# Filter generation in a diffusion-trunk kernel: the middle sample's spreading matmuls replaced by one spread per group, and absolute values of sample tiles added on GpSimd

## The chip, the cores and the metric

The kernel runs on one core of a Trainium2 chip. Five engines work side by side and meet through semaphores: TensorE (PE in the trace) multiplies matrices, VectorE (DVE), ScalarE (ACT) and GpSimd (POOL) work on tiles of 128 partitions, and SyncE (SP) issues the transfers between memory and the core. The metric is the device time of one execution in microseconds (us), the median of several runs.

## The reference, cut to what matters

The whole trunk is one layer for two request groups (a prompt of 256 rows, a sample of 1024): modulation, a projection, neighbourhood attention beside a long convolution, an output projection, and a routed mixture of experts. Only the first part of the kernel is touched: it makes the spectra of the convolution's filters, for both lengths and both orders.

```python
def implicit_filter_fft(length, w1, b1, w2, b2, w3, freq):
    ...
    hid = jnp.sin(fr * (z @ w1 + b1))
    hid = jnp.sin(fr * (hid @ w2 + b2))
    filt = (hid @ w3).reshape(length, 2, HYENA_ORDER, D_HYENA)
    filt = filt * window[:, None, None, :]
    fwd, bwd = filt[:, 0], filt[:, 1]
    two_sided = jnp.concatenate([fwd, zeros, bwd[1:][::-1]], axis=0)
    two_sided = two_sided / jnp.sum(jnp.abs(two_sided), axis=0, keepdims=True)
    return jnp.fft.rfft(two_sided, axis=0)
```

The spectrum also takes up the convolution's skip term (`hyena_bias`), since adding `u * bias` after the convolution is adding the bias to each cosine coefficient.

## The kernel before

The kernel is a row of phases with a barrier between them: filters, projection, attention, convolution (`hyena`), mixing and routing, experts. The filters phase fills the span's first 324 us and the projection starts after its barrier; nothing of the projection runs before that.

Inside `filters` each engine has a fixed program, written out by hand, and runs it in order. Its pieces:

- **Units** 0 to 9 are tiles of filter samples: for order 0 unit 0 is the prompt (t = -1) and 1 to 4 the sample (t = 0 to 3); for order 1 they are 5 and 6 to 9. For a unit, PE makes four 128x512 results (`gen`), DVE multiplies them by the window tile (`windowed`, into `AB`; with three small operations more where t is 0 or -1), POOL adds and subtracts `AB` into the operand tile `opnd` (three operations, `s_pool`), DVE adds one more (`odd_sine`), ACT takes two absolute values (`absolute`, into `MA` and `MB`), and DVE takes the larger of them (`larger`, into `MA`). `MA` and `MB` are one buffer each.
- **Sums.** For each unit PE multiplies `MA` by a matrix of ones and accumulates in `pn` (`sums`, two matmuls). `close` adds the middle sample's share. DVE takes the reciprocal of `pn` (`inverse`, into `rn`). There are four groups: order 0 prompt (0), order 0 sample (1), order 1 prompt (2), order 1 sample (3). ACT may overwrite `MA` only when PE has summed it.
- **Spectra.** Group g has jobs j: 5 for a prompt, 17 for the sample; below, spectrum 1/6 is job 6 of group 1. PE multiplies the basis table by `opnd` (one matmul for a prompt, four for a sample) into `pk`, which has two buffers. For jobs whose coefficients see the middle sample (3 of 5, 9 of 17) PE adds two matmuls of one row each, a rounded part `mid_h` and a rest `mid_l` times the signs `sgn`. DVE (`spectrum_out`) scales `pk` by `rn`, for cosines adds the skip term in a second operation, and writes `spec`, also of two buffers, which SP stores; DVE waits for the store before the last. PE waits for DVE's job before the last.
- **Ada.** Between these, 24 steps of the modulation: SP loads 1 MB, PE multiplies, DVE copies out. PE's step waits for DVE's last one.

On PE the order is gen 2, sums 1, ada, spectra 0/0 to 0/4, gen 3, sums 2, ada, gen 4, sums 3, ada, sums 4, close 1, then spectra 1/0 to 1/16 with gen 5 to 9 after jobs 0, 3, 6, 9, 12 (`GEN_AT`), sums 5 to 9 after jobs 2, 5, 8, 11, 14 (`SUM_AT`) and close 2 and 3 after jobs 2 and 14; then groups 2 and 3. SP loads a window tile only in its turn between the stores (`win_load`), behind an ada load and a table load.

## Time and profile before

| | us |
|---|---|
| median of three runs | 3416.4 |
| lowest and highest | 3412.28, 3417.86 |
| profiled execution, device time | 3407.46 |
| its span in the trace | 3405.7 |

The profile shows one execution; its device time is 1.8 us above its span and 8.9 us under the median. Over the whole span PE is busy 94%, DVE 65%, ACT 49% and GpSimd 11%. The trace gives each instruction's start and duration from the span's start. An idle time in brackets names what ended it. The granted clock is TensorE's, as a share of 2.4 GHz: 1.00 is 2.4 GHz, 0.50 is 1.2 GHz. A float32 matmul is two records in the trace, one of the rounded type is one.

### The profile page before, as it was taken

Reading aid. Unit: us, or ns where it says so; the run is one execution under the profiler, and the core shown is the slowest. Engines: PE = TensorE matmul, PEld = TensorE weight load, DVE = VectorE, ACT = ScalarE, POOL = GpSimd, SP = SyncE. Lnnn points to the kernel's source line nnn. Section 1 sums busy time; section 2 is a strip of 40 time slices with the busy share of each in tenths; the row PEclk is TensorE's granted clock in tenths of the full one; section 3 lists DMA queues with packets and bytes.
Section 4 is the critical chain, followed back from the end, with each engine's and each line's share of the span. In section 5 each row is a group of like instructions: output and inputs, shape, how many; then the busy total and the mean of one; then the engine's idle time right before and its main releaser. Section 6 shows DMA issues by size and latency. Waiting matters only on the chain.

```text
span 3405.7 us, 54105 instructions
## 1 busy us (share of the span) xinstructions
PE 3194.1 (94%) x22270; PEld 2430.2 (71%) x22270; DVE 2196.7 (65%) x2820; ACT 1655.7 (49%) x2154; POOL 373.3 (11%) x316
## 2 busy tenths in 40 slices
PE   4898999979899894999999999999999999999996
PEld 2443788878778773777777777777777777777774
DVE  6643333167666547777777777777777777777775
ACT  1102322156412333666666666666666666666663
POOL 1210100011244131000000000000000000000010
PEclk8999999989999896999999999999999999999998
DMA  3465342254676434788778778777777777777785
GB/s 138 182 221 195 99 128 94 72 146 126 223 245 218 150 101 165 278 299 293 273 289 298 274 285 295 275 288 289 278 289 281 281 291 280 285 283 289 277 325 200
DMA packets 226034, 791.14 MB, mean 232 GB/s; under 512 B 28525, under 2 KB 35321, under 8 KB 221564
## 3 DMA queue, kind: packets, MB, share of 16 engines
q1 hardware_dynamic: 206028, 722.02, 57.3%
q0 software_dynamic: 19760, 65.65, 6.7%
q8 instruction: 177, 2.90, 0.3%
q14 instruction: 69, 0.57, 0.0%
HBM read 730.31 MB, written 57.26 MB: 231 GB/s over the span
## 4 chain that ended last, share of the span: by engine, by line
PE 58%; DMA 1%; DVE 1%; ACT 0%; issue 0%; POOL 0%; SPq 0%; ACTq 0%; POOLq 0%; DVEq 0%
PE exp_bank L2779 15%; PE exp_bank L2781 14%; PE exp_bank L2780 14%; PE exp_bank L2789 14%; PE exp_bank L2761 1%; DMA out_y<-exp_xb 1%; PE exp_bank L2763 1%; DMA exp_xb<-residual 0%; PE exp_bank L2747 0%; DVE g_pick L2342 0%; DVE g_pick L2341 0%; DVE g_pick L2344 0%; DVE exp_lo L2475 0%; DMA exp_xq<-hidden_rows,g_rows_q 0%; PE exp_bank L2751 0%
## 5 line engine op out<-in xcount | busy, mean ns | idle before, releaser
L2475 DVE TENSOR_TENSOR exp_lo<-exp_raw,exp_hi 128x1024 fp32r<-128x1024 f32 x1056 | 1277.4, 1223 | 249.4 <-ACT exp_hi L2471 191.0
L2471 ACT ACTIVATE exp_hi<-exp_raw 128x1024 fp32r<-128x1024 f32 x1056 | 1119.2, 1061 | 572.0 <-PE exp_bank L2781 558.4
L2779 PE MATMUL exp_bank<-exp_hi,exp_xt 128*128 128x512 f32 (+1 forms) x1536 | 588.6, 383 | 1.3 <-DVE exp_xt L2628 1.0
L2781 PE MATMUL exp_bank<-exp_hi,exp_xt 128*128 128x512 f32 (+1 forms) x1536 | 571.9, 372 | 0.0
L2780 PE MATMUL exp_bank<-exp_lo,exp_xt 128*128 128x512 f32 (+1 forms) x1536 | 571.4, 372 | 0.0
L2779 PEld LDWEIGHTS exp_bank<-exp_hi,exp_xt 128*128 128x128 f32 x1536 | 289.4, 188 | 86.9 <-issue 39.1
L2781 PEld LDWEIGHTS exp_bank<-exp_hi,exp_xt 128*128 128x128 f32 x1536 | 289.6, 189 | 52.0
L2789 PE MATMUL exp_bank<-exp_raw,exp_xtp 128*32 128x256 f32 (+1 forms) x6144 | 324.1, 363 | 0.0
L2780 PEld LDWEIGHTS exp_bank<-exp_lo,exp_xt 128*128 128x128 f32 x1536 | 290.2, 189 | 45.4
L2779 PE MATMUL exp_bank<-exp_hi,exp_hid 128*128 128x512 f32 x704 | 283.7, 403 | 10.4 <-DVE exp_lo L2475 10.4
L2781 PE MATMUL exp_bank<-exp_hi,exp_hid 128*128 128x512 f32 x704 | 275.8, 392 | 0.0
L2789 PEld LDWEIGHTS exp_bank<-exp_raw,exp_xtp 128*32 128x32 f32 x6144 | 185.2, 110 | 127.0 <-issue 30.9
L2780 PE MATMUL exp_bank<-exp_lo,exp_hid 128*128 128x512 f32 x704 | 275.3, 391 | 0.0
L503 PE MATMUL proj_bank<-proj_hh,proj_hi 128*128 128x512 f32 (+1 forms) x480 | 170.0, 354 | 2.0 <-DVE proj_lo L126 2.0
L504 PE MATMUL proj_bank<-proj_hl,proj_hi 128*128 128x512 f32 (+1 forms) x480 | 170.0, 354 | 0.0
L2779 PEld LDWEIGHTS exp_bank<-exp_hi,exp_hid 128*128 128x128 f32 x704 | 132.6, 188 | 52.3 <-issue 16.3
L505 PE MATMUL proj_bank<-proj_hh,proj_lo 128*128 128x512 f32 (+1 forms) x480 | 169.8, 354 | 0.0
L2789 PE MATMUL exp_bank<-exp_raw,exp_hidp 128*32 128x256 f32 x2816 | 162.3, 381 | 0.0
L2520 POOL TENSOR_TENSOR exp_step<-g_ident 1x1 f32<-1x1 f32 x16 | 4.0, 250 | 1422.3 <-PE exp_bank L2751 1391.1
L2781 PEld LDWEIGHTS exp_bank<-exp_hi,exp_hid 128*128 128x128 f32 x704 | 132.7, 188 | 28.8
L2780 PEld LDWEIGHTS exp_bank<-exp_lo,exp_hid 128*128 128x128 f32 x704 | 132.9, 189 | 25.5
L1167 PE MATMUL filt_pk<-filt_opnd,filt_table 128*128 128x512 f32 x292 | 136.9, 611 | 8.2 <-DVE filt_spec L1379 8.0
(407 smaller groups left out, 4294.0 us busy)
## 6 DMA issues: line engine op xcount, KB each, us to landing
exp_raw<-in_w SPq DMA_DIRECT2D x1056, 512.0 KB
hy_table<-in_basis_s POOLq DMA_DIRECT2D x64, 512.0 KB
carry_tiles<-in_w_ada SPq DMA_DIRECT2D x24, 1024.0 KB, 5.6
proj_raw<-in_w_in SPq DMA_DIRECT2D x24, 512.0 KB
filt_table<-in_kbasis_s SPq DMA_DIRECT2D x18, 512.0 KB, 6.3
spectrum_s<-filt_spec SPq DMA_DIRECT2D x34, 256.0 KB, 2.4
carry_flex<-spectrum_s SPq DMA_DIRECT2D x16, 512.0 KB
features<-proj_xr SPq DMA_DIRECT2D x12, 512.0 KB, 3.0
```

What stands on the lines that cost most here:

```text
L503: pe.matmul(out, whi, hh[:, k, c0:c0 + w], start=(k == 0), stop=False)
L504: pe.matmul(out, whi, hl[:, k, c0:c0 + w], start=False, stop=False)
L505: mm = pe.matmul(out, wlo, hh[:, k, c0:c0 + w], start=False, stop=(k == KT - 1))
L1167: mm = pe.matmul(pk[n % 2][:], table[:, c % NR, ti * 128:(ti + 1) * 128], opnd[:, at, x, :], start=(t == 0), stop=(t == nt - 1 and not rank1))
L2471: act.activation(st.hi[:, n % st.ns, :], raw(n), ACT.Copy).then_inc(st.hi_done, 1)
L2475: dve.tensor_tensor(st.lo[:, n % st.ns, :], raw(n), st.hi[:, n % st.ns, :].bitcast(F32), ALU.subtract).then_inc(st.lo_done, 1)
L2761: pe.transpose(turn_s[:, i * 128:(i + 1) * 128], hd[:, i * 128:(i + 1) * 128], g["ident"][:])
L2763: tr = pe.transpose(turn_p[:, i * 128:(i + 1) * 128], hdp[:, i * 128:(i + 1) * 128], g["ident"][:])
L2779: pe.matmul(out, xh, wh, start=(k == 0), stop=False)
L2780: pe.matmul(out, xh, wl, start=False, stop=False)
L2781: mm = pe.matmul(out, xl, wh, start=False, stop=(k == nk - 1))
L2789: mm = pe.matmul(banks(e * NU + i)[2][q * CAP_P:(q + 1) * CAP_P, 0:w], x[:, k, :], raw(e * NC + c)[:, base + q * w:base + q * w + w], star ...
```

## The change

The middle sample is no longer added by PE in each job. Instead, once, eight float32 matmuls of one row (`middle_rows`) spread it for the four groups into `pk`, ACT copies each result into `spread`, and DVE multiplies it by `rn` and adds the skip term to its cosine half (`fold`, three operations a group). `spectrum_out` then adds the folded tile instead of the skip term; sine jobs that see the middle sample get a second operation that they did not have. For sample units t = 1 to 3 GpSimd adds `MA` to a running total (`totals`), which unit t = 0 starts, and PE sums each group once (sums 0, 4, 5, 9). Sums 4 and close 1 move behind spectrum 1/0.

```diff
+    SUM_AT = {2: 5, 14: 9}
     CLOSE_AT = {2: 2, 14: 3}
...
             def sums(n):
                 gi = group(n)
-                first = n == 0 or group(n - 1) != gi
-                pe.wait_ge(s_MA, n + 1)
-                if first and gi:
+                if UNITS[n][1] < 0:
+                    src = MA
+                    pe.wait_ge(s_MA, n + 1)
+                else:
+                    src = totals[UNITS[n][0]]
+                    pe.wait_ge(s_acc, adds(n))
+                if gi:
                     pe.wait_ge(s_rn, gi)
                 for m in range(2):
-                    mm = pe.matmul(pn[:], g["ones"][:], MA[:, m, :], start=(first and m == 0), stop=False)
+                    mm = pe.matmul(pn[:], g["ones"][:], src[:, m, :], start=(m == 0), stop=False)
                 mm.then_inc(s_sum, 1)
 
             def close(gi):
                 if gi == 0:
                     pe.wait_ge(s_ma, 1)
                 pe.matmul(pn[:], g["ones"][ones_at(gi), :], mid_a[ones_at(gi), :], start=False, stop=True).then_inc(s_n, 1)
+
+            def middle_rows():
+                pe.wait_ge(s_mf, 4)
+                for k in range(8):
+                    gi, x = divmod(k, 2)
+                    if k >= 2:
+                        pe.wait_ge(s_spo, k - 1)
+                    pe.matmul(pk[k % 2][:], sgn[ones_at(gi), :], midf[ones_at(gi), x, :], start=True, stop=True).then_inc(s_sp, 1)
...
-                rank1 = with_middle(q, j)
                 nt = MT if q else 1
                 for t in range(nt):
                     ti, at = ((j % 2) * MT + t, o * PER + 1 + t) if q else (j, o * PER)
                     mm = pe.matmul(pk[n % 2][:], table[:, c % NR, ti * 128:(ti + 1) * 128], opnd[:, at, x, :],
-                                   start=(t == 0), stop=(t == nt - 1 and not rank1))
-                if closes(q, j):
-                    mm.then_inc(s_used, 1)
-                    if not rank1:
-                        return
-                if rank1:
-                    gi, s = 2 * o + q, int(kind == "sin")
-                    pe.matmul(pk[n % 2][:], sgn[ones_at(gi), :], mid_h[ones_at(gi), s, :], start=False, stop=False)
-                    mm = pe.matmul(pk[n % 2][:], sgn[ones_at(gi), :], mid_l[ones_at(gi), s, :], start=False, stop=True)
-                mm.then_inc(s_k, 1)
+                                   start=(t == 0), stop=(t == nt - 1))
+                mm.then_inc(s_used if closes(q, j) else s_k, 1)
...
             gen(2)
-            sums(1)
+            middle_rows()
             ada()
             for j in range(NJ[0]):
                 spectrum(0, 0, j)
             gen(3)
-            sums(2)
             ada()
             gen(4)
-            sums(3)
             ada()
-            sums(4)
-            close(1)
             for j in range(NJ[1]):
                 spectrum(0, 1, j)
+                if j == 0:
+                    sums(4)
+                    close(1)
                 if j in GEN_AT:
                     gen(GEN_AT[j])
...
@@ -1248,8 +1258,11 @@
                 for s, out in enumerate((MA, MB[:])):
                     act.wait_ge(s_AB, 2 * n + s + 1)
                     if n:
-                        act.wait_ge(s_sum, n)
                         act.wait_ge(s_MA, n)
+                        if UNITS[n - 1][1] < 0:
+                            act.wait_ge(s_sum, 1 if n == 1 else 3)
+                        elif added(n - 1):
+                            act.wait_ge(s_acc, adds(n - 1))
...
             absolute(0)
             absolute(1)
-            act.wait_ge(s_mf, 4)
-            act.activation(mid_h[:], midf[:], ACT.Copy).then_inc(s_mh, 1)
+            for k in range(8):
+                act.wait_ge(s_sp, k + 1)
+                act.activation(spread[:, k // 2, k % 2, :], pk[k % 2][:], ACT.Copy).then_inc(s_spo, 1)
             for n in range(2, len(UNITS)):
                 absolute(n)
...
                     if s == 0:
                         ins = pool.tensor_tensor(opnd[:, n, 1, :], AB[:, 0, :], AB[:, 1, :], ALU.subtract)
                     ins.then_inc(s_pool, 1)
+                if added(n):
+                    pool.wait_ge(s_MA, n + 1)
+                    if adds(n) % (MT - 1) != 1:
+                        pool.wait_ge(s_acc, adds(n) - 1)
+                    pool.tensor_tensor(totals[UNITS[n][0]], totals[UNITS[n][0]], MA, ALU.add).then_inc(s_acc, 1)
...
             def larger(n):
                 dve.wait_ge(s_abs, 2 * n + 2)
-                dve.tensor_tensor(MA, MA, MB[:], ALU.max).then_inc(s_MA, 1)
+                first = UNITS[n][1] == 0
+                dve.tensor_tensor(totals[UNITS[n][0]] if first else MA, MA, MB[:], ALU.max).then_inc(s_MA, 1)
 
             def inverse(gi):
                 dve.wait_ge(s_n, gi + 1)
                 if gi == 0:
                     dve.wait_ge(s_mf, 4)
                 dve.reciprocal(rn[:, gi, :], pn[:]).then_inc(s_rn, 1)
+                if gi:
+                    fold(gi)
+
+            def fold(gi):
+                if gi == 0:
+                    dve.wait_ge(s_skip, 32)
+                dve.wait_ge(s_rn, gi + 1)
+                dve.wait_ge(s_spo, 2 * gi + 2)
+                dve.tensor_tensor(spread[:, gi, 0, :], spread[:, gi, 0, :], rn[:, gi, :], ALU.mult).then_inc(s_fold, 1)
+                dve.tensor_tensor(spread[:, gi, 1, :], spread[:, gi, 1, :], rn[:, gi, :], ALU.mult).then_inc(s_fold, 1)
+                dve.wait_ge(s_fold, 3 * gi + 1)
+                dve.tensor_tensor(spread[:, gi, 0, :], spread[:, gi, 0, :], skip[:, gi // 2, :], ALU.add).then_inc(s_fold, 1)
...
+                if kind != "sin" or with_middle(q, j):
+                    if not with_middle(q, j):
+                        term = skip[:, o, :]
+                    else:
+                        dve.wait_ge(s_fold, 3 * (2 * o + q) + 3)
+                        term = spread[:, 2 * o + q, int(kind == "sin"), :]
                     chain(ins)
-                    ins = dve.scalar_tensor_tensor(spec[:, n % 2, :], skip[:, o, :], col, spec[:, n % 2, :], ALU.mult, ALU.add)
+                    ins = dve.scalar_tensor_tensor(spec[:, n % 2, :], term, col, spec[:, n % 2, :], ALU.mult, ALU.add)
                 ins.then_inc(s_ev, 1)
...
-            dve.wait_ge(s_mh, 1)
-            dve.tensor_tensor(mid_l[:], midf[:], mid_h[:].bitcast(F32), ALU.subtract).then_inc(s_ml, 1)
             inverse(0)
             ada()
             unit(2)
             ada()
+            fold(0)
             for j in range(NJ[0]):
                 spectrum_out(0, 0, j)
```

Three places where the order of instructions changes, as they stand on their engines.

ScalarE, between the absolute values of unit 1 and those of unit 2 (`filt_hid` holds `MA`), before:

```order
L1256 ACTIVATE filt_hid<-filt_AB 128x1024 [waits filt_abs_ready,filt_abs_summed,filt_ab_ready]
L1256 ACTIVATE filt_MB<-filt_AB 128x1024 [waits filt_abs_ready,filt_abs_summed,filt_ab_ready]
L1271 ACTIVATE filt_mid_h<-filt_spec 128x1024 [waits filt_mid_ready]
L1256 ACTIVATE filt_hid<-filt_AB 128x1024 [waits filt_abs_ready,filt_abs_summed,filt_ab_ready]
L1256 ACTIVATE filt_MB<-filt_AB 128x1024 [waits filt_abs_ready,filt_abs_summed,filt_ab_ready]
```

and now:

```order
L1269 ACTIVATE filt_hid<-filt_AB 128x1024 [waits filt_abs_summed,filt_abs_ready,filt_ab_ready]
L1269 ACTIVATE filt_MB<-filt_AB 128x1024 [waits filt_abs_summed,filt_abs_ready,filt_ab_ready]
L1285 ACTIVATE filt_spread<-filt_pk 128x512 [waits filt_mid_spread] x8
L1269 ACTIVATE filt_hid<-filt_AB 128x1024 [waits filt_abs_ready,filt_ab_ready]
L1269 ACTIVATE filt_MB<-filt_AB 128x1024 [waits filt_abs_ready,filt_ab_ready]
```

Eight copies from PSUM stand ahead of unit 2's absolute values, where one copy from SBUF stood; the wait for PE's sums is gone there.

GpSimd, from unit 3's third operation on, before:

```order
L1285 TENSOR_TENSOR filt_opnd<-filt_AB 128x512 [waits filt_ab_ready] x2
L1287 TENSOR_TENSOR filt_opnd<-filt_AB 128x512
L1285 TENSOR_TENSOR filt_opnd<-filt_AB 128x512 [waits filt_ab_ready] x2
L1287 TENSOR_TENSOR filt_opnd<-filt_AB 128x512
L1285 TENSOR_TENSOR filt_opnd<-filt_AB 128x512 [waits filt_ab_ready] x2
```

and now (`filt_opnd<-filt_opnd,filt_hid` is the add into the total):

```order
L1299 TENSOR_TENSOR filt_opnd<-filt_AB 128x512 [waits filt_ab_ready]
L1307 TENSOR_TENSOR filt_opnd<-filt_opnd,filt_hid 128x1024 [waits filt_abs_added,filt_abs_ready]
L1299 TENSOR_TENSOR filt_opnd<-filt_AB 128x512 [waits filt_ab_ready]
L1301 TENSOR_TENSOR filt_opnd<-filt_AB 128x512
L1299 TENSOR_TENSOR filt_opnd<-filt_AB 128x512 [waits filt_ab_ready]
```

An add of 128x1024 that waits for DVE's maximum now stands between one unit's operations and the next one's; the same holds for units 2, 4, 7, 8 and 9.

TensorE, at the first sample spectrum (1/0, line 1167 before and 1187 now), before:

```order
L1141 MATMUL filt_pn<-filt_hid,g_ones 128x512 [waits filt_abs_ready]
L1141 MATMUL filt_pn<-filt_hid,g_ones 128x512
L1147 MATMUL filt_pn<-g_pick,g_ones 128x512
L1167 MATMUL filt_pk<-filt_opnd,filt_table 128x512 [waits filt_odd_sine,filt_spec_ready,filt_mixed,filt_table_landed1]
L1167 MATMUL filt_pk<-filt_opnd,filt_table 128x512 x3
L1175 MATMUL filt_pk<-filt_mid_h,filt_sgn 128x512
L1176 MATMUL filt_pk<-filt_mid_l,filt_sgn 128x512
```

and now:

```order
L1187 MATMUL filt_pk<-filt_opnd,filt_table 128x512 [waits filt_odd_sine,filt_spec_ready,filt_mixed,filt_table_landed1]
L1187 MATMUL filt_pk<-filt_opnd,filt_table 128x512 x3
L1154 MATMUL filt_pn<-filt_opnd,g_ones 128x512 [waits filt_rnorm,filt_abs_added]
L1154 MATMUL filt_pn<-filt_opnd,g_ones 128x512
L1160 MATMUL filt_pn<-g_pick,g_ones 128x512
L1128 MATMUL filt_pf<-filt_W,filt_hs 128x512 [waits filt_ab_ready,filt_hid_lo]
```

The sum and the closing matmul of group 1 now follow spectrum 1/0 where they preceded it, and DVE's reciprocal, which ends in `rn` for job 1/0, follows them.

## Rows read from the trace of the kernel before

**Rows 1.** Top line of the page: the profiled span.

```profile
span 3405.7 us, 54105 instructions
```

**Rows 2.** Busy by stretch: length, engines' us, granted clock, DMA.

```profile
122.27:160.38 38.11, 36.30 (x141) 16.91 (x140) 29.37 (x35) 4.01 (x4) 10.57 (x6) 1.00 0.37 131
160.38:232.56 72.18, 69.87 (x259) 31.53 (x255) 38.07 (x60) 6.35 (x6) 15.54 (x9) 1.00 0.60 216
232.56:317.65 85.09, 83.50 (x343) 37.06 (x342) 25.92 (x63) 8.39 (x14) 0.00 (x0) 0.96 0.57 204
```

**Rows 3.** Timeline of PE, 175 to 181: start, duration, line, tiles, idle before.

```profile
175.00 1.88 PE L1141 MATMUL filt_pn<-filt_hid,g_ones 128*128 128x512 f32 x4
176.72 3.60 PE L1167 MATMUL filt_pk<-filt_opnd,filt_table 128*128 128x512 f32 x8
180.25 0.49 PE L1175 MATMUL filt_pk<-filt_mid_h,filt_sgn 1*128 1x512 f32 x1
...
180.89 0.50 PE L1119 MATMUL filt_pf<-filt_W,filt_hs 128*128 128x512 f32 x1
```

**Rows 4.** Groups by line: the middle's spreading matmuls, over the whole run.

```profile
L1175 PE MATMUL filt_pk<-filt_mid_h,filt_sgn 1*128 1x512 f32 x24 | 12.1, 506 | 0.0
```

**Rows 5.** Groups by line, then two timeline rows: nearest prices of added work.

```profile
L1968 POOL TENSOR_TENSOR carry_flex<-carry_flex 128x1024 f32<-128x1024 f32 x10 | 23.8, 2379 | 160.0 <-DVE carry_flex L2098 160.0
L2557 ACT ACTIVATE exp_xt<-exp_bank 128x512 fp32r<-128x512 f32 x32 | 17.2, 585 | 26.4 <-PE exp_bank L2747 26.4
77.23 0.69 DVE L1415 TENSOR_TENSOR g_pick<-filt_spec,g_pick 128x512 f32<-128x512 f32 x1
88.44 1.06 ACT L1256 ACTIVATE filt_hid<-filt_AB 128x1024 f32<-128x1024 f32 x1 [11.61 <-PE filt_pn L1141]
```

**Rows 6.** Timeline of POOL and PE around the last unit before spectrum 1/0.

```profile
113.79 1.28 POOL L1285 TENSOR_TENSOR filt_opnd<-filt_AB 128x512 f32<-128x512 f32 x1 [3.18 <-DVE filt_AB L1340]
...
116.72 2.24 POOL L1285 TENSOR_TENSOR filt_opnd<-filt_AB 128x512 f32<-128x512 f32 x1
117.90 3.39 PE L1141 MATMUL filt_pn<-filt_hid,g_ones 128*128 128x512 f32 x4 [2.49 <-DVE filt_hid L1355]
121.22 1.12 PE L1147 MATMUL filt_pn<-g_pick,g_ones 1*128 1x512 f32 x2
122.27 3.70 PE L1167 MATMUL filt_pk<-filt_opnd,filt_table 128*128 128x512 f32 x8
```

**Rows 7.** Timeline of DVE: first group, first sample spectra, units 5 and 6.

```profile
92.09 0.74 DVE L1376 SCALAR_TENSOR_TENSOR filt_spec<-filt_pk,filt_rowf,filt_rn 128x512 f32<-128x512 f32 x1
...
98.43 0.75 DVE L1376 SCALAR_TENSOR_TENSOR filt_spec<-filt_pk,filt_rowf,filt_rn 128x512 f32<-128x512 f32 x1 [4.16 <-DMA spectrum_p<-filt_spec]
...
110.83 1.23 DVE L1355 TENSOR_TENSOR filt_hid<-filt_hid,filt_MB 128x1024 f32<-128x1024 f32 x1 [1.36 <-ACT filt_MB L1256]
...
122.38 3.36 DVE L1361 RECIPROCAL filt_rn<-filt_pn 128x512 f32<-128x512 f32 x1 [4.07 <-PE filt_pn L1147]
...
128.12 2.47 DVE L1340 TENSOR_TENSOR filt_AB<-filt_pf,filt_win 128x512 f32<-128x512 f32 x4
...
133.83 2.17 DVE L1355 TENSOR_TENSOR filt_hid<-filt_hid,filt_MB 128x1024 f32<-128x1024 f32 x1
...
145.89 2.48 DVE L1340 TENSOR_TENSOR filt_AB<-filt_pf,filt_win 128x512 f32<-128x512 f32 x4 [0.80 <-DMA filt_win<-in_win_s]
```

**Rows 8.** Granted clock in short stretches, and the PE row after the idle.

```profile
101.00:104.00 3.00, 3.00 (x7) 1.36 (x6) 0.91 (x2) 0.00 (x0) 0.00 (x0) 0.50 0.40 152
...
107.00:110.00 3.00, 3.00 (x25) 1.35 (x23) 2.44 (x3) 1.21 (x2) 3.00 (x3) 0.98 0.27 112
...
100.02 1.85 PE L1167 MATMUL filt_pk<-filt_opnd,filt_table 128*128 128x512 f32 x2 [3.71 <-DVE filt_spec L1379]
```

**Rows 9.** Timeline of DVE where a store has to land first.

```profile
229.26 0.75 DVE L1376 SCALAR_TENSOR_TENSOR filt_spec<-filt_pk,filt_rowf,filt_rn 128x512 f32<-128x512 f32 x1 [1.79 <-DMA spectrum_p<-filt_spec]
...
296.25 0.75 DVE L1376 SCALAR_TENSOR_TENSOR filt_spec<-filt_pk,filt_rowf,filt_rn 128x512 f32<-128x512 f32 x1 [6.61 <-DMA spectrum_s<-filt_spec]
```

25 lines of the change are left out of this document (14 added, 11 removed).

## The prediction

> **What bounds the kernel now.** I read the page's top line first: the profiled span is 3405.7 us [rows 1] of a device time of 3407.46. The filters phase ends before the next phase starts, so only this phase can move the time, and what it gains or loses at its end goes straight into the total. Then the table by stretch [rows 2]: from the first sample spectrum (1/0, at 122.27) to 160.38 PE is busy 36.3 of 38.1 us, from there to the end of group 2 69.9 of 72.2, and to the last spectrum 83.5 of 85.1, at a granted clock of 1.00, 1.00 and 0.96. PE bounds these 195 us. But DVE is busy 29.4 us of the first 38.1, so it is the next bound there, and the timeline shows how tight it is: unit 6 on DVE waits for its window tile [rows 7], and a store holds DVE up twice [rows 9]. Ahead of 122.27 PE waits for others: 3.71 us before spectrum 0/4 [rows 8], 2.49 before sums 4 [rows 6].
>
> **What the change takes off PE.** A pair of the middle's matmuls takes 0.64 us of PE (180.25 to 180.89) and a unit's sum 1.72 (175.00 to 176.72) [rows 3]. There are 24 pairs [rows 4], 3 of them in group 0, so 21 after 122.27: 13.4 us. Sums 6, 7 and 8 go too: 5.2. Taken at face value that is 18.6 us of a stretch that PE bounds. What follows walks the new program through, to see how much of it arrives.
>
> **Until spectrum 1/0: +3.3 us.** After gen 2, at 86.3, PE runs eight float32 matmuls of one row. The nearest rows are close's, 1.05 us each (121.22 to 122.27) [rows 6], and a spectrum's, 0.9 (3.60 for four) [rows 3]: 7.2 to 8.4, I take 7.6, till 93.9. The eight ACT copies (0.59 each [rows 5]) follow two buffers behind and hide under them, but the last ends at 94.5, and unit 2's absolute values, which stand behind them on ACT, come then: two of 1.06 [rows 5], the maximum (1.23 [rows 7]), the ada copy (0.5). Now fold 0: three operations of 0.69 [rows 5], which meet GpSimd's add of unit 2 (2.38 alone [rows 5]). Reading both operands from SBUF they wait for it; between none and all of it I take all: 102.2, where job 0/0 began at 92.09 [rows 7]. Part returns: DVE waited 4.16 for the first store then [rows 7], behind loads that are now over, and 2.4 should do. So spectrum 0/4 starts on PE at 107.7 instead of 100.02 [rows 8]; gen 3, without its pair, is 6.5 late. Sums 2 and 3 are gone, and unit 3's maximum ends at 117.7, where it was 112.06 (110.83 plus 1.23) [rows 7]. Here GpSimd gets into the path: its add for unit 3 runs until 120.3, and only then do unit 4's three operations start. They took 5.2 (113.79 to 118.96) [rows 6], so they end at 125.6, and spectrum 1/0 waits for them. Before, it started at 122.27 [rows 6].
>
> **From 1/0 to 1/6: +11.8 to +18.** Sums 4 and close 1 now come after spectrum 1/0: 3.6, 1.8 and 1.05 [rows 3, 6], so DVE's reciprocal starts at 132.1, not at 122.38 [rows 7]. It takes 3.36, fold 1 adds 2.1, job 1/0 1.5, so unit 5 starts at 139.2 where it was 128.12, 11.1 late [rows 7]. DVE needs 7.8 us for it (128.12 to 135.9) [rows 7] and is done at 147.0. PE meanwhile does gen 5, 1/1, ada and 1/2 until 142.9 and must then wait 4.2 us for unit 5's maximum, since sums 5 stands after 1/2. Then sum, close, 1/3: 153.6. Unit 6 needs its window tile, whose load SP issues behind an ada load and a table load; the gap from those to its arrival is the one that ended at 145.89 [rows 7], 8.8 us, and gives 156.8. Unit 6 takes 7.8, reciprocal and fold 5.5, the ada copy 0.5: 170.6. PE's ada step after 1/5 waits for that copy, idle since 164.1, and 1/6 starts at 172.2 with job 1/4 done. Before: 160.38, so +11.8.
>
> The clock can add to it. After PE had idled 3.71 us it stood at 0.50, 1.2 GHz, from 101 to 104 and was back at 0.98 from 107 on [rows 8]: some 7 us of work at half speed. After 2.49 us of idle the two matmuls of sums 4 took 3.3 (117.90 to 121.22) [rows 6] for the usual 1.7. The new program has three gaps, of 5.9 us (119.7 to 125.6), 4.2 and 4 to 6.5. Each should cost what these two did, 1.6 to 3.4. Two of them lie on the chain whole, and of the third 1.4: up to +18, the window's lateness then hidden.
>
> **From 1/6 to the end of group 2: -0.6 to +0.7.** Here 4.5 us of pairs and 3.5 of sums leave PE, out of 72.2 [rows 2]. But units 7 to 9 wait on DVE for window tiles (as at 145.89 [rows 7]) whose loads follow PE's and DVE's steps by the same 7 to 9 us, so DVE comes due 0.7 to 0.9 us after PE twice. Sums 9 waits for GpSimd: unit 9's three operations (5.2 [rows 6]) and then the add of 2.38 [rows 5] end 16.7 us after PE's ada step ahead of 1/12, where the sum stood at 14.6; that is 2.1 lost, not 0.6 gained. Fold 3 (2.1) falls between job 1/15 and job 1/16, and the prompt's jobs 2/0 to 2/4 go at the pace of stores [rows 9]; their four pairs (2.6) bring nothing, and DVE is 0.9 later. Sum: 71.6 for 72.2; with a slow clock at its start an estimated 1.3 more.
>
> **From there to the end: -4.5.** Nine pairs, 5.8 us, and DVE's additions (four operations of 0.75) have room. The stall at 296.25, where the first store behind six loads of 512 KB lands [rows 9], keeps its time and takes 1.3 of it back. The tail is unchanged.
>
> **Sum.** 11.8 - 0.6 - 4.5 = +6.7 at the low end, 18 + 0.7 - 4.5 = +14.2 at the high end. I take +11, nearer the high one, since rows 6 and 8 show the clock down after shorter gaps than the new ones. The profiled execution would go from 3407.5 to 3418.5, the median from 3416.4 to 3427.4.
>
> A rule against the change: the Trainium skill, "GPSIMD Engine Reference", section "4.1 Engine selection", wants two-input elementwise work on VectorE, GpSimd being about half as fast. The trace has 2.38 us for such an operation on GpSimd [rows 5] and 1.23 for the same size on DVE [rows 7]. With the adds on DVE the wait at 120.3 would be about 1.2 us shorter, and the result would be nearer +10.
>
> **The rivals.**
> *PE's relief arrives (faster).* If the waits of DVE, SP and GpSimd that I placed are slack in fact, the stretch after 122.27 shrinks by 18.6, by 1.8 of idle before sums 6, and gives back 1.3 at the loads, while 1/0 starts 3.3 late: -15.8, 3400.6. It decides at unit 5: it holds if the 11.1 us by which DVE is later there are made good before 1/6. For it: PE is 95% to 98% busy after 122.27 [rows 2]. Against: DVE is at 77% in the first stretch, and it gets 4.3 us more of folds just there.
> *The clock stays up (hardly slower).* If no gap lowers it, +6.7: 3423.1. Against it: rows 6 and 8.
> *The two cancel.* If only unit 5's lateness arrives and the loads and adds of 1/6 to 2/4 cost nothing, +6.7 less 5 to 7: about 3416 to 3418.
> *More contention.* If GpSimd's add also stops the second operation of cosine jobs and stretches DVE's folds each time (up to 2.38 for each of six adds), and every gap costs 3.4: +20 to +24, 3438.
> *It doesn't do what it says.* The instruction order shows pairs and sums gone, so none of the chance is here.
>
> **How the numbers follow.** 0.2% of the median is 6.8 us, about what a measurement of this kernel can tell from no change. Chances: forecast 0.50 (+7 to +15), clock stays up 0.12, cancel 0.15, relief arrives 0.14, more contention 0.09. Slower by over 0.2% (above 3423.2): all but a little of the first, all of the last, a little of the second: 0.60. Within it: 0.26. Faster: 0.14. The range leaves out the relief and the far end of the contention: 3408 to 3437. Of it, 3423 to 3431 is the forecast's own.
>
> **What would show it.** In the profile after: spectrum 1/0 on PE at about 125.6 (122.27 before); a wait of PE for DVE's maximum or GpSimd's add at sums 5 and sums 9; PE idle before the ada step ahead of 1/6, which should start at 172 to 178; PEclk under 1.00 between 125 and 185; the last spectrum's end at 324 to 332 instead of 317.65. The forecast is wrong if 1/6 starts before 165, or if PE shows no idle between 1/2 and sums 5; then the relief has arrived.

## The result, and the profile after

The changed kernel takes 3427.5 us (median of 6 runs, 3424.2 to 3434.3) against 3413.3 (6 runs, 3411.5 to 3417.9): a ratio of 1.0042, with a 95% interval of 1.0029 to 1.0055. That is slower by 14 us. The prediction started from a median of 3416.4 (3 runs); with six runs it is 3413.3. The profiled execution took 3430.9 us with a span of 3429.1. I profiled each kernel a second time later: before took 3416.1 there and the changed one 3426.9.

How far can one trace be trusted? In both traces of before the last spectrum ends at 317.7, though the executions differ by 8.6 us. That difference arose behind this phase, where no version changes anything: from the end of the last spectrum to the end of the execution before took 3089.8 and 3098.4 us, the changed kernel 3091.5 and 3090.8. What sets this scatter stays open. The end of the last spectrum on PE is therefore the sharper measure of what the phase costs, and the table goes by it. The columns between are the starts of DVE's three big reciprocals, one behind each of close 1, 2 and 3; they divide the phase in four.

| kernel | 1/0 on PE | recip 1 | recip 2 | recip 3 | last spectrum ends |
|---|---|---|---|---|---|
| before, two traces | 122.3 / 119.5 | 122.4 / 119.6 | 153.7 / 151.0 | 217.8 / 215.1 | 317.7 / 317.7 |
| after, two traces | 127.3 / 127.5 | 136.8 / 136.3 | 171.4 / 170.6 | 242.1 / 243.7 | 339.4 / 336.1 |

By the means of two, the change is 15.6 us late at recip 1, 18.6 at recip 2, 26.4 at recip 3, and 20.0 at the end: the last stretch is the only one that gains. The phase thus loses 20 us where the medians lose 14.

The windows that answer to [rows 2] (columns as there: length; PE, weight loads, DVE, ACT, POOL busy; granted clock, DMA share, GB/s) run from the old start of 1/0 to the new, to 1/6, to the end of group 2, to the last spectrum:

```profile
122.27:127.28 5.01, 0.00 (x0) 0.03 (x1) 2.65 (x5) 1.91 (x2) 5.01 (x4) 0.50 0.83 314
127.28:179.51 52.23, 43.67 (x137) 18.95 (x137) 33.03 (x41) 4.01 (x4) 12.75 (x7) 0.83 0.26 91
179.51:257.40 77.89, 67.20 (x244) 30.92 (x244) 47.73 (x68) 6.35 (x6) 22.91 (x12) 0.90 0.56 202
257.40:339.35 81.95, 77.41 (x320) 35.13 (x308) 28.49 (x67) 8.38 (x14) 0.00 (x0) 0.94 0.60 212
```

PE was busy 36.3 of 38.1 us between 1/0 and 1/6 at a clock of 1.00. Now it is busy 43.7 of 52.2, at 0.83: there is less work in the stretch, and it has both more idle time and longer matmuls. DVE's busy time from 1/6 to the end of group 2 rose from 38.1 to 47.7, with eight instructions more: fold 3's three (2.1 us) and five second operations of sine jobs at 0.75. That is 5.8 of the 9.7; the rest is waiting inside instructions, of which the next rows show cases.

The timeline of PE at its gaps (start, duration, line, tiles, idle before and what ended it):

```profile
86.23 10.17 PE L1168 MATMUL filt_pk<-filt_spec,filt_sgn 1*128 1x512 f32 x16
...
127.28 6.70 PE L1187 MATMUL filt_pk<-filt_opnd,filt_table 128*128 128x512 f32 x8 [5.71 <-POOL filt_opnd L1299]
...
151.43 3.78 PE L1154 MATMUL filt_pn<-filt_hid,g_ones 128*128 128x512 f32 x4 [4.01 <-DVE filt_hid L1375]
...
177.16 0.61 PE L1105 MATMUL filt_pa<-filt_sel,g_pick 128*128 128x2 f32 x4 [4.34 <-DVE g_pick L1324]
```

These are the three gaps the prediction named: ahead of 1/0, ahead of sums 5, and ahead of the ada step before 1/6. Spectrum 1/0 took 6.70 us where it took 3.70 before [rows 6]. The first row is the eight spreading matmuls, at 10.17 us instead of the 7.6 I had put down.

The timelines of GpSimd and of DVE at the first add, and DVE at two later ones:

```profile
100.26 2.34 POOL L1307 TENSOR_TENSOR filt_opnd<-filt_opnd,filt_hid 128x1024 f32<-128x1024 f32 x1 [9.56 <-DVE filt_hid L1375]
100.56 2.59 DVE L1390 TENSOR_TENSOR filt_spread<-filt_spread,filt_rn 128x512 f32<-128x512 f32 x1
140.18 0.69 DVE L1390 TENSOR_TENSOR filt_spread<-filt_spread,filt_rn 128x512 f32<-128x512 f32 x1
...
195.08 2.17 DVE L1415 SCALAR_TENSOR_TENSOR filt_spec<-filt_kz,filt_rowf,filt_spec 128x512 f32<-128x512 f32 x1
198.58 0.75 DVE L1415 SCALAR_TENSOR_TENSOR filt_spec<-filt_spread,filt_rowf,filt_spec 128x512 f32<-128x512 f32 x1
```

The fold's multiplication takes 0.69 alone and 2.59 while the add runs: it ends at 103.15, half a microsecond behind the add's end at 102.60. The second operation of a cosine job, 0.75 alone, takes 2.17 in the same way, and 2.83 at 209.97. Both read two operands from SBUF. (The Trainium skill, "SBUF — State Buffer", section "Who interferes with whom", says that a DVE instruction with two SBUF inputs contends with a GpSimd instruction that reads SBUF, and that the port pair they share is an exclusive lock; these rows agree.)

A stopped operation also holds up transfers, since SP issues its work in order. The timelines of SP and POOL, then of PE at sums 9:

```profile
197.27 0.33 SPq L1028 DMA_DIRECT2D spectrum_s<-filt_spec  x1
197.65 0.43 SPq L1014 DMA_DIRECT2D filt_win<-in_win_s  x1
...
229.33 2.79 POOL L1307 TENSOR_TENSOR filt_opnd<-filt_opnd,filt_hid 128x1024 f32<-128x1024 f32 x1
...
232.17 3.62 PE L1154 MATMUL filt_pn<-filt_opnd,g_ones 128*128 128x512 f32 x4 [2.45 <-POOL filt_opnd L1307]
```

The operation that started at 195.08 ends at 197.25; only then can its store go, and the window load of unit 8 is issued behind that store. The load of unit 9 follows, at 215.69, the store of the one stopped at 209.97. Unit 9's maximum ends at 228.24; its add, which stands behind three other operations on GpSimd, ends 3.9 us later, and sums 9 wait for it.

### The profile page after: what moved, and what is told of

Same layout as the page of the kernel before. It is cut to its first block, busy times and chain, and to the rows that moved or that the text cites. A ratio compares the mean times of both kernels' runs of the same rounds, so it can differ in the third digit from the quotient of the medians.

```text
span 3429.1 us, 54057 instructions
## 1 busy us (share of the span) xinstructions
PE 3199.8 (93%) x22214; PEld 2434.6 (71%) x22214; DVE 2215.9 (65%) x2841; ACT 1658.4 (48%) x2159; POOL 388.3 (11%) x322
## 4 chain that ended last, share of the span: by engine, by line
PE 59%; DVE 1%; DMA 1%; ACT 0%; POOL 0%; issue 0%; SPq 0%; ACTq 0%; POOLq 0%; DVEq 0%
PE exp_bank L2814 15%; PE exp_bank L2816 14%; PE exp_bank L2815 14%; PE exp_bank L2824 14%; PE exp_bank L2796 1%; DMA out_y<-exp_xb 1%; PE exp_bank L2798 1%; PE exp_bank L2782 0%; DVE g_pick L2377 0%; DVE g_pick L2376 0%; DVE g_pick L2379 0%; DMA exp_xq<-hidden_rows,g_rows_q 0%; DMA exp_xb<-residual 0%; PE exp_bank L2786 0%; POOL exp_xg L2556 0%
## 5 line engine op out<-in xcount | busy, mean ns | idle before, releaser
L2816 PEld LDWEIGHTS exp_bank<-exp_hi,exp_xt 128*128 128x128 f32 x1536 | 289.9, 189 | 52.2
L504 PE MATMUL proj_bank<-proj_hl,proj_hi 128*128 128x512 f32 (+1 forms) x480 | 170.6, 355 | 0.0
L1187 PE MATMUL filt_pk<-filt_opnd,filt_table 128*128 128x512 f32 x292 | 150.0, 665 | 18.7 <-DVE filt_spec L1415 13.0
```

The costliest lines, as they stand in the source:

```text
L504: pe.matmul(out, whi, hl[:, k, c0:c0 + w], start=False, stop=False)
L1187: mm = pe.matmul(pk[n % 2][:], table[:, c % NR, ti * 128:(ti + 1) * 128], opnd[:, at, x, :], start=(t == 0), stop=(t == nt - 1))
L2816: mm = pe.matmul(out, xl, wh, start=False, stop=(k == nk - 1))
```

## The experiments

Times are medians; every interval is the 95% one of the ratio to before. "End" is the end of the last spectrum on PE.

### The two halves apart

The fold half alone keeps the spreading, the folds and the spectra without pairs; each unit's sums go back to PE:

```
-    SUM_AT = {2: 5, 14: 9}
+    SUM_AT = {2: 5, 5: 6, 8: 7, 11: 8, 14: 9}
...
-                    pool.tensor_tensor(totals[UNITS[n][0]], totals[UNITS[n][0]], MA, ALU.add).then_inc(s_acc, 1)
```

> The fold half alone: the middle sample is spread once per group and folded into the skip term, while every unit's absolute values go to PE's sums again, in their places of before (sums 4 and close 1 ahead of 1/0). My theory (the loss comes from GpSimd's adds, which block DVE and hold up ACT, and from the late close 1) expects 1/0 at 125 to 127, unit 5 on DVE at 132 to 135 instead of 143.5, 1/6 at 165 to 169 instead of 179.5, and then the pairs' 4.5 us back in the last stretch: 3411 to 3418. The rival (the eight one-row matmuls with their copies, and the folds on DVE, carry the loss) expects it as slow as the changed kernel, 3424 or more. If pairs on PE were all that counted, 3400 to 3405.

Measured: 3412.4 us, ratio 1.0001 (0.9992 to 1.0009). Spectrum 1/0 at 129.7, unit 5 at 136.5, 1/6 at 173.0, end at 321.9. The time came out as my theory had it, but the places did not: 1/0 and unit 5 were 3 and 2 us above my ranges, 1/6 was 12.7 us late, not 5 to 9, and the last stretch gave back 7.2, not 4.5. By the phase's end the half is not neutral: it is 4.2 us later than before. So part of the rival holds too: of the changed kernel's lateness at recip 1 this half has 8.8 us without any add.

The adds half alone keeps the pairs and the old handling of the middle:

```
                 for m in range(2):
-                    mm = pe.matmul(pn[:], g["ones"][:], MA[:, m, :], start=(first and m == 0), stop=False)
+                    mm = pe.matmul(pn[:], g["ones"][:], src[:, m, :], start=(m == 0), stop=False)
...
+                    pool.tensor_tensor(totals[UNITS[n][0]], totals[UNITS[n][0]], MA, ALU.add).then_inc(s_acc, 1)
```

> The adds half alone: the middle's pairs stay in the spectra, GpSimd adds the absolute values, sums 1 to 3 and 6 to 8 go, and sums 4 with close 1 stand behind 1/0. My theory: 1/0 starts at 120 to 122, since nothing delays group 0, but recip starts at 127 to 129 instead of 122.38, so unit 5 is about 5 us late and 1/6 at 165 to 169 instead of 160.38; sums 9 waits for the add. Time 3417 to 3423, a loss that nothing pays back. The rival (the adds are harmless because GpSimd is idle there): 5.2 us of sums less, 3407 to 3410.

Measured: 3421.9 us, ratio 1.0023 (1.0013 to 1.0032). 1/0 at 119.2, recip 1 at 128.7, unit 5 at 133.6, 1/6 at 164.6, end at 326.1. Recip 1 is the whole loss: it is 7.7 us later than the mean of before although 1/0 is no later, because close 1 now stands behind 1/0, and 1/0 itself takes 5.85 us after an idle of 5.37 where it took 3.70. The harmless-adds rival is out.

| | recip 1 | recip 1 to 2 | recip 2 to 3 | recip 3 to end |
|---|---|---|---|---|
| before (means) | 121.0 | 31.4 | 64.1 | 101.2 |
| fold alone | 129.8 | 33.6 | 64.5 | 94.0 |
| adds alone | 128.7 | 30.5 | 66.4 | 100.5 |
| both (means) | 136.6 | 34.4 | 71.9 | 94.8 |

The halves' lateness at recip 1 adds up (8.8 and 7.7, together 16.5, measured 15.6). Between recip 2 and 3 it doesn't: 0.4 and 2.3 alone, 7.8 together. The gain behind recip 3 belongs to the fold: 7.2 us there against 0.7.

What the two do to each other between recip 2 and 3 is taken apart below, behind the run with three adds.

### Close 1 back in its place, and PE kept busy

```
             ada()
+            sums(4)
+            close(1)
             for j in range(NJ[1]):
                 spectrum(0, 1, j)
-                if j == 0:
-                    sums(4)
-                    close(1)
```

> The changed kernel with one thing moved: sums 4 and close 1 stand ahead of 1/0 again. 1/0 then starts 4 to 5 us later than 127.28, and recip at 131 to 133 instead of 136.8. My theory (DVE's chain recip, fold, unit 5, unit 6 sets 1/6) expects unit 5 at 138 to 140 and 1/6 some 3 to 5 us earlier: 3422 to 3425. The rival (PE's own work and its slow clock set 1/6) expects the 4 us lost ahead of 1/0 to stay: 3427 to 3431.

Measured: 3424.2 us, ratio 1.0032 (1.0019 to 1.0045), inside my range, but the interval overlaps the changed kernel's. 1/0 fell to 134.4, 7.1 us later than in the changed kernel and not 4 to 5, and yet recip 1 came at 134.5 instead of 136.8, unit 5 at 141.2 (both somewhat above my ranges), 1/6 at 175.2 (179.5), end at 334.1. A later 1/0 with an earlier 1/6: what sets 1/6 hangs on the reciprocal, not on the start of 1/0. Of the 4.3 us gained, 2.3 come at recip 1; the rest comes at unit 6, which waits for its window tile here (158.9) and for PE's gen 6 in the changed kernel (163.5).

The same question from the other side, matmuls that nobody reads in PE's three gaps:

```
+            def fill(n, count):
+                pe.wait_ge(s_AB, 2 * n + 2)
+                for _ in range(count):
+                    pe.matmul(pf[0][:], g["ones"][:], opnd[:, 1, 0, :], start=True, stop=True)
```

> The changed kernel with idle PE kept busy: plain float32 matmuls whose result nobody reads, six ahead of 1/0, four ahead of sums 5, four ahead of the ada step after 1/5 (each about 0.9 us at full clock). If the clock after the gaps is a cost of its own, the granted clock stays near 1.00 from 123 to 133 and from 151 to 160, and the time falls by 3 to 8 us: 3419 to 3424. If the gaps cost only their length, or the fill itself is in the way of the chain, 3427 to 3433.

Measured: 3425.6 us, ratio 1.0036 (1.0023 to 1.0049). The windows from 122 to 130 and from 130 to 180 (PE busy, clock, DMA):

```profile
122.00:130.00 8.00, 7.78 (x11) 0.61 0.55 197
130.00:180.00 50.00, 44.97 (x155) 0.96 0.29 105
```

The clock was up from 130 on, 0.96 against 0.84 in the same window of the changed kernel, and 1/0 took 3.60 us again. Nevertheless recip 1 came at 136.9 and 1/6 at 179.1, where they were at 136.8 and 179.5 (178.9 in the second trace); the end, at 341.6, was no earlier. The six matmuls ahead of 1/0 themselves took 8.41 us at the low clock and cost the first gap's gain, so this run doesn't price that gap. It prices the second, at unit 6 on DVE, here and then in the changed kernel:

```profile
162.76 2.48 DVE L1369 TENSOR_TENSOR filt_AB<-filt_pf,filt_win 128x512 f32<-128x512 f32 x4 [3.79 <-DMA filt_win<-in_win_s]
```

```profile
163.55 2.48 DVE L1359 TENSOR_TENSOR filt_AB<-filt_pf,filt_win 128x512 f32<-128x512 f32 x4 [0.17 <-PE filt_pf L1129]
```

With the clock up, PE's gen 6 is done by 160.1 and DVE idles 3.79 us until the window tile lands. In the changed kernel gen 6 came last, at 163.5 in this trace and in time for 162.77 in the second. So the low clock behind the second gap cost 0 to 0.8 us: the window tile was due by then, whose load SP issues 17.6 us behind the start of recip 1 in both kernels. The third was filled only until 171.9, 4.5 us ahead of the ada step, and 1/6 still took 5.56 us, so the clock's cost behind it stays open. The median is 1.9 us under the changed kernel's, less than the two intervals can tell apart.

### The eight spreading matmuls

With 32 partitions contracted, 31 of them zero:

```
-                    pe.matmul(pk[k % 2][:], sgn[ones_at(gi), :], midf[ones_at(gi), x, :], start=True, stop=True).then_inc(s_sp, 1)
+                    pe.matmul(pk[k % 2][:], sgn[32 * gi:32 * gi + 32, :], midf[32 * gi:32 * gi + 32, x, :], start=True, stop=True).then_inc(s_sp, 1)
```

> The changed kernel, with the eight matmuls that spread the middle sample contracted over 32 partitions instead of one (31 of them hold zeros, so the result is the same). In the changed kernel they took 10.17 us and the granted clock fell from 1.00 to 0.50 while they ran back to back. If it fell because one row is too little work, it stays at 1.00 here: the eight take 7.2 to 7.8 us, 0/0 is some 2.5 us earlier, and the time 3423 to 3427. If it falls all the same, the engine's waits for ACT's copies or something else brought it down, and nothing changes: 3427 to 3430.

Measured: 3426.6 us, ratio 1.0042 (1.0028 to 1.0055); the eight took 10.15 us. No effect. With all 128 partitions contracted (`sgn[:, :]`, `midf[:, x, :]`):

> The changed kernel with the eight spreading matmuls contracted over all 128 partitions. The middle samples of all four groups are summed in them, so what is spread is not one group's value: a kernel for timing alone. With 32 rows the clock fell as with one (10.15 us for the eight). If few rows in use is what brings it down, all 128 keep it at 1.00 and the eight take 7 to 8 us, and the time is 3422 to 3426. If it is the rhythm with ACT's copies or what went before, the clock falls here too, and the time stays at 3426 to 3429.

Measured: 3424.1 us, ratio 1.0031 (1.0021 to 1.0041). The eight in the timeline, and the window from 90 to 94 (PE busy, clock, DMA), for all 128 rows:

```profile
86.08 7.31 PE L1168 MATMUL filt_pk<-filt_spec,filt_sgn 128*128 128x512 f32 x16
90.00:94.00 4.00, 4.00 (x20) 1.00 0.00 0
```

and for 32 rows:

```profile
86.47 10.15 PE L1168 MATMUL filt_pk<-filt_spec,filt_sgn 32*128 32x512 f32 x16
90.00:94.00 4.00, 4.00 (x8) 0.50 0.00 0
```

The order, the waits and ACT's copies are the same in all three kernels, and PE shows no idle in any. With 1 or 32 rows the clock went from 2.4 to 1.2 GHz in the middle of the eight; with 128 it stayed at 2.4. What came ahead of the eight and the rhythm of the copies are therefore out as causes: of the two readings given for this run, the number of rows in use holds. Between 32 and 128 rows nothing was run. Recip 1 came 3.1 us earlier (133.5), as the 2.9 us shorter matmuls have it, and recip 2 3.0 us (167.9 against the mean of 171.0); at the end (336.5) nothing was left of it.

### The adds on DVE

```
+                if added(n):
+                    dve.wait_ge(s_MA, n + 1)
...
+                    dve.tensor_tensor(totals[UNITS[n][0]], totals[UNITS[n][0]], MA, ALU.add).then_inc(s_acc, 1)
```

> The changed kernel with the adds on DVE, right behind each maximum, instead of on GpSimd (1.23 us each where GpSimd took 2.35, and no operation of DVE is held up by GpSimd). The prediction put that at 1.2 us ahead of 1/0 and the result near +10, which is 3426. If what GpSimd does to DVE and ACT is worth more than the adds' own time on DVE: 1/0 starts at 124 to 126 instead of 127.28 and the time is 3419 to 3424. If DVE is the bound all along, six adds of 1.23 are paid there and the time is 3427 to 3432.

Measured: 3424.9 us, ratio 1.0044 (1.0030 to 1.0057). 1/0 at 127.6, recip 1 at 136.9, end at 333.2. Ahead of recip 1 nothing is gained: GpSimd's hold is gone, but two of the three adds took 2.17 us on DVE itself (118.42 and 126.41), beside GpSimd's mixing. The end is 3 to 6 us earlier, the ratio isn't. The gain lies between recip 2 and 3, which took 68.7 us for the changed kernel's 71.9: sums 9 wait 0.69 us instead of 2.45 and 3.88, and the clock stays up behind them. In the time, these runs don't decide between "near +10" and no difference.

### The rows where PE is idle

The fold half again. The middle's values lie in group 3's part of `spread`, which is overwritten last; group 0's two matmuls come behind gen 2, four more ahead of sums 4 and two ahead of sums 6; unit 2's absolute values go ahead of the copies:

```
-            middle_rows()
+            pe.wait_ge(s_mf, 4)
+            middle_rows((0, 1), pk)
...
+            pe.wait_ge(s_AB, 10)
+            middle_rows((2, 3, 4, 5), pf)
             sums(4)
...
             for n in range(2, len(UNITS)):
                 absolute(n)
+                if n == 2:
+                    spreads((0, 1), pk)
```

> The fold half alone again, with the middle sample spread where PE is idle: two matmuls for group 0 behind gen 2, and their two copies behind unit 2's absolute values on ACT; four for groups 1 and 2 ahead of sums 4, two for group 3 ahead of sums 6. My theory (the fold half gains nothing because eight matmuls and eight copies stand ahead of unit 2's absolute values and make group 0, and with it close 1, 7 us late) expects larger 2 to end at 92 to 94 instead of 101.2, 1/0 at 123 to 126 instead of 129.7, and a time of 3403 to 3408, faster than before. The rival (the folds on DVE and the window loads set 1/6 anyway) expects 3410 to 3413.

Measured: **3401.4 us, ratio 0.9974 (0.9963 to 0.9985)**: faster than before, by 9 us by the ratio, and below my range of 3403 to 3408. The timeline of PE:

```profile
88.35 1.98 PE L1163 MATMUL filt_pk<-filt_spread,filt_sgn 1*128 1x512 f32 x4
...
116.27 1.99 PE L1163 MATMUL filt_pf<-filt_spread,filt_sgn 1*128 1x512 f32 x8
118.84 1.99 PE L1152 MATMUL filt_pn<-filt_hid,g_ones 128*128 128x512 f32 x4 [0.57 <-DVE filt_hid L1377]
120.75 1.12 PE L1158 MATMUL filt_pn<-g_pick,g_ones 1*128 1x512 f32 x2
121.80 3.70 PE L1182 MATMUL filt_pk<-filt_opnd,filt_table 128*128 128x512 f32 x8
```

The rows ahead of sums 4 stand where PE had idled 2.49 us [rows 6], and sums 4 took 1.99 us instead of 3.39. The four of them, two for group 1 and two for group 2, take 1.99 us together, as long as group 0's two at 88.35. Recip 1 is at 121.9, recip 2 at 154.2, recip 3 at 217.6, where before's traces have 119.6 to 122.4, 151.0 to 153.7 and 215.1 to 217.8; the end is at 310.5, 7.2 us earlier. So the 13.4 us of pairs taken off PE arrive only behind recip 3. Ahead of it, DVE's units 6 to 9 each wait for their window tile, 2.3 to 3.6 us where they waited 0.8 to 2.6 in before's first trace: the window loads hold the pace when PE is relieved. The folds go on top there, and relief of PE pays for them at best.

Then the folds on GpSimd (the function `fold` word for word, with `pool` for `dve`, called behind the mix of units 2, 4, 6 and 9):

> The kernel with the rows spread late, and its twelve fold operations on GpSimd instead of DVE, each behind the mix of the group's last unit. My theory (DVE's chain from the reciprocal over the fold to unit 5 and unit 6 sets 1/6) expects unit 5 some 2 us and 1/6 some 3 to 4 us earlier, since DVE goes straight on to the next unit: 3400 to 3405. The rival (three operations of some 1.6 us on GpSimd end later than three of 0.69 on DVE, and the cosine job that reads them waits, with unit 5 behind it) expects 3 us lost per group: 3407 to 3415.

Measured: 3407.6 us, ratio 0.9980 (0.9971 to 0.9989); end at 311.0, like the version with the folds on DVE. It neither gains what my theory had, nor loses 3 us per group. Job 1/0's second operation waits for GpSimd, and unit 5 starts at 129.24 against 128.63:

```profile
128.57 0.75 DVE L1413 SCALAR_TENSOR_TENSOR filt_spec<-filt_spread,filt_rowf,filt_spec 128x512 f32<-128x512 f32 x1 [2.84 <-POOL filt_spread L1311]
```

The medians differ by 6 us where the phase's ends differ by 0.5, and the intervals of the two ratios overlap; that difference lies behind the phase, and I don't count it for either.

### Three adds, where close 1 doesn't hang on them

```
         def added(n):
-            return UNITS[n][1] > 0
+            return UNITS[n][0] == 1 and UNITS[n][1] > 0
```

on top of the kernel with the rows spread late: sums 6, 7 and 8 go, group 1 is untouched.

> The kernel with the rows spread late (3401), with GpSimd's adds for units 7 to 9 alone: sums 6, 7 and 8 go, sums 9 takes the total; group 1 keeps its four sums and close 1 its place. If the adds are only harmful where close 1 hangs on them and their unit is on the chain, the 5.2 us of sums off PE arrive in part: 3396 to 3401. If the wait of sums 9 for the last add and the blocked second operations of cosine jobs (0.8 to 2.1 us each) eat the relief: 3401 to 3405, and then the adds half pays nowhere in this kernel.

Measured: 3412.1 us, ratio 0.9995 (0.9986 to 1.0004), against 0.9974. Both theories said at most 3405. Up to recip 2 the two kernels are alike (154.3 and 154.2), at recip 3 this one is at 224.9 instead of 217.6, its end at 320.4 instead of 310.5. Taking 5.2 us of work off PE and giving GpSimd three adds cost 10 us. The timeline of PE, GpSimd and DVE, and the window from 190 to 205:

```profile
194.23 0.61 PE L1105 MATMUL filt_pa<-filt_sel,g_pick 128*128 128x2 f32 x4 [2.77 <-DVE g_pick L1339]
...
197.84 5.85 PE L1187 MATMUL filt_pk<-filt_opnd,filt_table 128*128 128x512 f32 x8 [1.75 <-DVE filt_spec L1427]
...
216.68 1.98 PE L1157 MATMUL filt_pn<-filt_opnd,g_ones 128*128 128x512 f32 x4 [2.75 <-POOL filt_opnd L1322]
...
194.79 2.35 POOL L1322 TENSOR_TENSOR filt_opnd<-filt_opnd,filt_hid 128x1024 f32<-128x1024 f32 x1
...
194.87 2.82 DVE L1427 SCALAR_TENSOR_TENSOR filt_spec<-filt_kz,filt_rowf,filt_spec 128x512 f32<-128x512 f32 x1
190.00:205.00 15.00, 10.48 (x39) 4.85 (x38) 10.35 (x16) 1.73 (x2) 7.14 (x4) 0.77 0.38 138
```

and the same window without the adds:

```profile
190.00:205.00 15.00, 14.48 (x61) 7.25 (x63) 8.36 (x16) 0.41 (x1) 3.39 (x2) 1.00 0.54 203
```

PE idles 2.77 us, where it had a sum to do, and waits for DVE; the add stops the cosine job's second operation for 2 us more (2.82 instead of 0.75); PE waits another 1.75 for it; the clock comes down, and the next spectrum takes 5.85 instead of 3.70. With all that PE is through with the spectrum ahead of sums 9 at 213.9, where sums 9 had begun at 209.3. But another chain is later still. The timelines of SP and of unit 9's start on DVE, with the adds:

```profile
197.72 1.85 SPq L1028 DMA_DIRECT2D spectrum_s<-filt_spec  x2
...
200.57 0.43 SPq L1014 DMA_DIRECT2D filt_win<-in_win_s  x1
207.34 2.48 DVE L1374 TENSOR_TENSOR filt_AB<-filt_pf,filt_win 128x512 f32<-128x512 f32 x4 [2.07 <-DMA filt_win<-in_win_s]
```

and without:

```profile
194.20 1.84 SPq L1028 DMA_DIRECT2D spectrum_s<-filt_spec  x2
...
197.06 0.43 SPq L1014 DMA_DIRECT2D filt_win<-in_win_s  x1
203.84 2.48 DVE L1362 TENSOR_TENSOR filt_AB<-filt_pf,filt_win 128x512 f32<-128x512 f32 x4 [3.02 <-DMA filt_win<-in_win_s]
```

The window load of unit 9 is issued 3.5 us late, behind the store that waits for the stopped operation, and unit 9 starts 3.5 us late. Its add then ends 3.9 us behind its maximum, and sums 9 start 7.4 us late (216.68 against 209.32). The stretch from recip 2 to recip 3, divided at DVE's units 7 and 9 and at PE's sums 9 (starts, us):

| | recip 2 to unit 7 | unit 7 to 9 | unit 9 to sums 9 | sums 9 to recip 3 |
|---|---|---|---|---|
| before (means) | 14.7 | 34.6 | 6.9 | 7.9 |
| fold alone | 17.3 | 33.5 | 5.6 | 8.1 |
| adds alone | 14.2 | 33.8 | 8.9 | 9.6 |
| both, two traces | 16.5 / 16.1 | 35.0 / 34.5 | 9.35 / 9.35 | 9.9 / 13.2 |
| both, adds on DVE | 16.1 | 36.7 | 7.7 | 8.2 |
| rows late | 16.0 | 33.7 | 5.5 | 8.2 |
| rows late, three adds | 17.1 | 36.0 | 9.3 | 8.2 |

Three things stand in it. First, where GpSimd adds and the pairs are gone, sums 9 start 9.3 us behind unit 9 each time, as GpSimd's three operations and the add have to be over; the relief of PE, worth 1.3 us there to the fold alone, can't show. Second, the clock behind that wait can be low, as in the second trace of the changed kernel:

```profile
230.51 3.07 PE L1154 MATMUL filt_pn<-filt_opnd,g_ones 128*128 128x512 f32 x4 [3.88 <-POOL filt_opnd L1307]
233.51 2.07 PE L1160 MATMUL filt_pn<-g_pick,g_ones 1*128 1x512 f32 x2
235.51 6.66 PE L1187 MATMUL filt_pk<-filt_opnd,filt_table 128*128 128x512 f32 x8
```

There 13.2 us pass to recip 3 instead of 8.2. Third, units 7 to 9 take about 1 us longer with both than with either half; in this run it is 2.3, and the two stopped operations ahead of the window loads (2.17 and 2.82 us instead of 0.75) are the cause that the rows show. So of the 7.4 us up to recip 3, GpSimd's queue has 3.9 and units 7 to 9 have 2.3; the last 1.2 were lost ahead of unit 7, before any add, and stay open. PE's gaps and its slow clock lay 2.75 us under this chain. Whether the missing sums alone would have cost something, no run shows. Another 2.5 us are lost behind recip 3; there the last five spectra take 19.04 us after an idle of 2.36, and 17.41 after one of 1.67 in the kernel without the adds.

### Both kernels once more

> The kernel before once more, for a second profiled execution: the first one lay at 3407.5, under the median of 3413. I expect the end of the last spectrum within 5 us of 317.65, and 1/6 within 5 us of 160.38; that bounds how much of the difference between single traces is chance.

> The changed kernel once more, for a second profiled execution: the first one lay at 3430.9, over the median of 3427.5. I expect 1/0 at 126.5 to 128, 1/6 at 177 to 180 and the last spectrum's end at 334 to 340: the lateness before 1/6 is the same each time, and what varies lies in the stores and loads of the last stretch.

Their numbers stand in the first table. What was expected of 1/6 (157.7 and 178.9), the end of before and the end after came out. What I had not expected is that before's 1/0 may start at 119.5 as well as at 122.3, and end the phase at the same time: 2.8 us gained early are gone at the end. The same happened to the 3 us of the run with 128 rows.

## The prediction, point by point

**Direction, size.** Slower, by 14.2 us in the medians where 11 was forecast; the time lay inside the forecast's own 3423 to 3431. That 3427.4 was forecast and 3427.5 measured is luck: the kernel before came out 3.1 us below the median the forecast started from, and some 6 us of the phase's loss don't appear in the medians. The phase itself lost 18.4 to 21.7 us in the pairs of traces, more than the sum's upper end of 14.2, so terms were missed, and the agreement of the total is better than that of its terms.

**Until 1/0: forecast +3.3, measured +5.0** from the trace the sum was made against (+8.0 by the second pair). The chain was the one named: ACT's copies, unit 2's absolute values, fold 0 held for the whole add, store, gen 3, add, mix. The term that was too small is the eight matmuls, 10.17 us for 7.6. They were priced at the high clock from rows of 1.05 and 0.9 each, and the clock fell under them. Unit 3's maximum, due at 117.7, ended at 118.6 and GpSimd's add at 122.1 instead of 120.3; the order of waits was right. That this term is real the kernel with the rows spread late shows: with the eight matmuls and copies out of the way of unit 2's absolute values, recip 1 is at 121.9 instead of the fold half's 129.8, and so where it was before.

**1/0 to 1/6: forecast +11.8 to +18, measured +14.1** (52.2 for 38.1; second traces 51.5 for 38.2). Gaps of 5.7, 4.0 and 4.3 us were forecast at 5.9, 4.2 and 4 to 6.5. The clock's part behind the first gap came as drawn: 1/0 took 3.0 us too long, and close 1 behind it was late by that. With 1/0's start 1.7 us later than forecast, it put unit 5 at 143.5 where 139.2 was forecast. What the filled gaps correct is the second: the clock was low there too, but it cost 0.8 us at most, because the window tile of unit 6 was due at nearly the same time. The step "two of them lie on the chain whole" holds for the first gap and not for the second; of the third it is open.

**1/6 to the end of group 2: forecast -0.6 to +0.7, measured +5.7** (77.9 for 72.2; second traces 79.7 for 73.6). This is the step that failed. I had DVE due 0.7 to 0.9 us after PE twice and 2.1 us lost at sums 9, and set 8 us of relief against it. The wait at sums 9 came: 2.4 us more than before pass between unit 9 and sums 9. What failed is the rest of the sum. The clock behind that wait stood in it at nothing, and cost 2.0 us in the first trace and 5.3 in the second (9.9 and 13.2 us from sums 9 to recip 3, for 7.9). And the relief didn't arrive: units 7 to 9 took 34.8 us for 34.6, where the two kernels with the pairs gone and no adds took 33.5 and 33.7. I had put the blocking of cosine jobs into a rival of 9%, as if it were a separate case; here it stopped two of their second operations by 1.4 and 2.1 us, with the window loads of units 8 and 9 issued behind them. That this is what ate the 1.2 us is likely from the rows and not shown by a run of its own.

**To the last spectrum: forecast -4.5, measured -3.1** by the first pair (82.0 for 85.1) and -9.0 by the second (77.4 for 86.4). The relief arrives here, as said, and somewhat more of it: the store's stall, forecast to keep its length, went from 6.61 to 6.77 and from 6.25 to 4.88. The two traces of the changed kernel differ here by 4.6 us, of which that stall is 1.9; another 1.7 are the last five spectra, which took 19.10 us after an idle of 2.81 and 17.41 after one of 0.92. The prediction had no clock in this stretch.

**The rivals.** That PE's relief arrives everywhere (3400.6) was wrong for this kernel; its condition, unit 5 on time at no cost, is met only by spreading the rows late, without the adds, and that kernel takes 3401.4. That this is so near the rival's number is chance: it keeps the sums on PE, and its gain ahead of recip 3 is nil. That the clock stays up, and that the effects cancel, are out by the windows and by 1/6. More contention (3438) had the right mechanism for the third stretch. The waits inside DVE's instructions come to some 6 us (1.9 at fold 0, then 1.4, 2.1 and 0.8 at cosine jobs), where it had up to 2.38 for each of six adds; the phase lost its +20 all the same, since the wait of sums 9 for the last add and the clock behind it come on top.

**The adds on VectorE.** The forecast was about 1 us less; the run lies 2.6 us lower in the median and equal in the ratio. It doesn't contradict the forecast and doesn't confirm it.

## What to carry over

Work on the bounding engine is worth removing only in stretches where no other engine or load is due at the same moment; here 13.4 us of pairs brought 7 us, all of it in the last stretch, and taking 5.2 us of sums off PE brought a loss, since the last of the adds that replaced them ends later than PE would have needed. When work must be added ahead of a tight chain, put it into gaps that already exist on its engine and behind what others wait for: the same eight matmuls and copies, moved, turned the fold half from no gain into 9 us. When an operation goes to GpSimd, look on DVE for instructions with two SBUF operands in the same microseconds, at the stores that wait for them and the loads that are issued behind these stores, and on GpSimd for what is queued behind.
